# A 31-tap convolution on three engines: ScalarE's tap products against GpSimd and VectorE doing all taps

## The reference, cut to what matters

```python
def hybrid_mix(h, ...):
    p = h @ w_in                               # 21 tiles of 128 channels
    ...
    y_a = gate_b * causal_depthwise_conv(gate_c * xa, sc_conv_w)      # 3 taps
    y_b = spatial_gating(u, v, sg_w, sg_b, sg_ln_w, sg_ln_b)
    y_c = rwkv7_time_mix(pc, ...)
    z1, z2 = jnp.split(pd, 2, axis=-1)
    zd = causal_depthwise_conv(z1 * jax.nn.sigmoid(z2), cm_conv_w) + cm_conv_b   # 31 taps
    y_d = jax.nn.silu(layer_norm(zd, cm_ln_w, cm_ln_b))
    return jnp.concatenate([y_a, y_b, y_c, y_d], axis=-1) @ w_out
```

## Time and profile before

| What | Value |
|---|---|
| median of three executions | 2330.22 us |
| the profiled execution's own time | 2334.19 us |
| its span, first to last instruction | 2332.3 us |
| TensorE busy | 2225.5 us, 95% |
| VectorE busy | 492.4 us, 21% |
| ScalarE busy | 342.0 us, 15% |
| GpSimd busy | 101.4 us, 4% |
| mean granted clock of TensorE | 0.956 of full |
| chain that ended last | PE 92%, DVE 5%, ACT 1% |

### The profile page before, as it was taken

The page is one execution under the profiler, slowest core; times in us unless marked ns, Lnnn a source line. Parts: engine busy times, 40 slices in busy tenths (PEclk is TensorE's granted clock), DMA queues, the critical chain, the costliest instruction groups (busy, mean ns, idle before and its releaser), DMA issues.

```text
span 2332.3 us, 26353 instructions
## 1 busy us (share of the span) xinstructions
PE 2225.5 (95%) x10308; PEld 1757.5 (75%) x10308; DVE 492.4 (21%) x1056; ACT 342.0 (15%) x773; POOL 101.4 (4%) x132
## 2 busy tenths in 40 slices
PE   8978899999878999999999999999999999999998
PEld 6755788888756788877777886877687778867776
DVE  0336310012452200021000463100110015530001
ACT  1113210001111100020000351100110013511001
POOL 0000000000000000000000070000000001600000
PEclk9965999999879999999999999999999999989999
DMA  6410244444202344434444421544464444124443
GB/s 256 149 37 0 73 145 153 153 135 134 93 35 67 114 153 153 150 130 129 151 153 143 148 71 57 178 153 153 145 218 153 153 149 140 63 68 158 153 153 117
DMA packets 81584, 299.47 MB, mean 128 GB/s; under 512 B 9120, under 2 KB 9248, under 8 KB 81248
## 3 DMA queue, kind: packets, MB, share of 16 engines
q1 hardware_dynamic: 80352, 293.87, 38.1%
q0 software_dynamic: 1152, 4.45, 0.5%
HBM read 296.98 MB, written 1.05 MB: 128 GB/s over the span
## 4 chain that ended last, share of the span: by engine, by line
PE 92%; DVE 5%; ACT 1%; issue 1%; DVEq 1%; DMA 0%; ACTq 0%; SPq 0%
PE psum L284 46%; PE psum L469 12%; PE psum L266 10%; PE psum L724 7%; PE psum L1674 5%; PE psum L2161 3%; PE psum L441 2%; PE psum L425 2%; PE psum L1558 1%; PE psum L2479 1%; PE psum L350 1%; PE psum L1622 1%; PE psum L404 0%; DVE sq L578 0%; DVE x L582 0%
## 5 line engine op out<-in xcount | busy, mean ns | idle before, releaser
L284 PE MATMUL psum<-h,ring 128*128 128x256 f32 x2976 | 654.7, 379 | 0.0
L284 PEld LDWEIGHTS psum<-h,ring 128*128 128x128 f32 x2976 | 565.1, 190 | 105.7 <-issue 32.5
L284 PE MATMUL psum<-x,ring 128*128 128x256 f32 x1728 | 391.4, 384 | 17.9 <-ACT x L2510 7.1
L284 PEld LDWEIGHTS psum<-x,ring 128*128 128x128 f32 x1728 | 332.8, 193 | 66.5 <-issue 16.3
L266 PE MATMUL psum<-hid,ring 128*128 128x256 f32 x1024 | 231.1, 379 | 0.0
L266 PEld LDWEIGHTS psum<-hid,ring 128*128 128x128 f32 x1024 | 194.6, 190 | 26.5
L469 PE MATMUL psum<-ring,hid 128*128 128x512 f32 x448 | 201.4, 592 | 0.0
L523 ACT ACTIVATE hid_act<-psum 128x256 f32<-128x256 f32 x88 | 33.8, 384 | 783.1 <-PE psum L284 729.0
L469 PEld LDWEIGHTS psum<-ring,hid 128*128 128x128 f32 x448 | 85.1, 190 | 83.2 <-issue 80.4
L538 DVE TENSOR_TENSOR hid<-psum,hid_act 128x256 f32<-128x256 f32 x56 | 23.8, 425 | 568.8 <-ACT hid_act L523 568.8
L469 PE MATMUL psum<-ring,space 128*128 128x512 f32 x256 | 112.3, 592 | 0.0
(11 more groups left out here) (328 smaller groups left out, 1620.7 us busy)
## 6 DMA issues: line engine op xcount, KB each, us to landing
ring<-in_weights SPq DMA_DIRECT2D x552, 512.0 KB, 3.3
space<-in_gains POOLq DMA_DIRECT2D x6, 512.0 KB, 4.5
const<-in_consts SPq DMA_DIRECT2D x1, 1493.0 KB, 11.0
x<-in_x SPq DMA_DIRECT2D x1, 1024.0 KB, 4.9
out<-x SPq DMA_DIRECT2D x2, 512.0 KB, 2.6
space<-in_params POOLq DMA_DIRECT2D x2, 509.5 KB, 4.5
space<-in_params SPq DMA_DIRECT2D x1, 659.0 KB, 12.0
space<-in_positions SPq DMA_DIRECT2D x1, 128.0 KB, 13.7
```

The lines of the kernel that those rows point to most:

```text
L284: last = pe.matmul(out, unit[:, i, :], rhs[:, i, :], start=(i == 0), stop=(i == KD - 1), skip_group_check=True)
```

## The change

ScalarE's `products` and GpSimd's `add_products` go, with the two semaphores and the product buffers. GpSimd convolves tile 0 alone with the existing helper `conv(s.zs, "cm_conv_w", CMW, s.zd, 1)`: a tensor_scalar (multiply) for the first tap, then for each of 30 taps a tensor_scalar into one of two `pool_t` tiles, a drain and a tensor_tensor add into `zd`; last a drain and a tensor_scalar that adds the bias, which marks the new step `zd`. VectorE does all 31 taps of tile 1. The fifteen new ones stand in the product series: four ahead of the add `n1`, four between `n1` and `n2`, seven between `n2` and `n3`, so the mark `taps` moves there. TensorE waits for `zd` and `taps` where it waited for the adds; VectorE waits for `zd` ahead of `centre("zn", ...)` and no longer waits ahead of `n1`.

```diff
-OWN_TAPS, PRODUCTS = 16, 4
-ADDED = 2 * CMW - OWN_TAPS
+OWN_TAPS = 16
...
-        self.pool = Steps(sem("mixer_convolutions"), "zs0 ya")
-        self.product_ready, self.product_added = sem("tap_products_ready"), sem("tap_products_added")
+        self.pool = Steps(sem("mixer_convolutions"), "zd ya")
...
-        pe.wait_ge(s.product_added, (l + 1) * (ADDED - 1))
+        pe.wait_ge(*at(s.pool, "zd"))
+        pe.wait_ge(*at(s.dve, "taps"))
         channel_sums("zn", "sum", s.zd, 2)
         out_part(2, 0, 0)
...
-    def products(first, last):
...
-        products(0, 5)
         tiles_out(12, 14)
...
-        products(5, 11)
         tiles_out(14, 16)
         square("vn")
-        products(11, 18)
         tiles_out(16, 18)
-        products(18, 22)
         deviation("vn", 1)
-        products(22, 28)
         tiles_out(18, 20)
-        products(28, 33)
         act.wait_ge(*at(s.dve, "decayed"))
         copy_bank(2, flat(s.vn_tok), "v_norm_tok")
-        products(33, 37)
         tiles_out(20, PROJ2)
...
-        products(37, ADDED)
...
-        taps(12, OWN_TAPS).then_inc(*s.dve.mark("taps"))
+        taps(12, OWN_TAPS)
         tiles_out(15, 17)
...
-        dve.wait_ge(s.product_added, (l + 1) * (ADDED - 1))
+        taps(OWN_TAPS, 20)
         add("n1", 6, s.n[0], s.n[1])
+        taps(20, 24)
         add("n2", 6, s.n[1], s.n[0])
+        taps(24, CMW).then_inc(*s.dve.mark("taps"))
         add("n3", 6, s.n[0], s.n[1])
+        dve.wait_ge(*at(s.pool, "zd"))
         centre("zn", s.zd, 2)
...
-        pool.tensor_tensor(s.zs[:, 0, CMW - 1:], s.z[:, 0, :], s.sz[:, 0, :], ALU.mult).then_inc(*s.pool.mark("zs0"))
+        pool.tensor_tensor(s.zs[:, 0, CMW - 1:], s.z[:, 0, :], s.sz[:, 0, :], ALU.mult)
         pool.drain()
         pool.wait_ge(*at(s.dve, "zs1"))
         load_gain(3 * l + 1)
-
-        def add_products(first, last):
...
-        add_products(1, CMW)
-        pool.wait_ge(*at(s.dve, "taps"))
-        add_products(CMW, ADDED)
+        conv(s.zs, "cm_conv_w", CMW, s.zd, 1)
+        pool.drain()
+        pool.tensor_scalar(s.zd[:, 0, :], s.zd[:, 0, :], s.p("cm_conv_b", 0), None, ALU.add).then_inc(
+            *s.pool.mark("zd"))
```

More of the change, by code:

```diff
@@ L630, in __init__ @@
         self.kk_sq = self.m[8][:, 4:8, :].rearrange("p q t -> p (q t)")
-        self.product = self.m[9].rearrange("p q t -> p (q t)").rearrange("p (n t) -> p n t", t=T)
         self.on_tok = self.m[8][:, 0:4, :].rearrange("p q t -> p (q t)").rearrange("p (n c) -> p n c", n=2)
@@ L670, in __init__ @@
         self.dve = Steps(sem("mixer_elementwise"), [
-            "lora_in", "kk_sq", "zs1", "run", "vn.xc", "decayed", "rkr", "taps", "vn", "bonus", "yb",
+            "lora_in", "kk_sq", "zs1", "run", "vn.xc", "decayed", "rkr", "vn", "bonus", "yb",
             *tt("before", "far_st"), *tt("before_ts", "ak", "rb"), *tt("rk"), *tt("n0"), *tt("p2t"), *tt("n1"),
-            *tt("n2"), *tt("n3"), "zn.xc", *tt("x1"), "zn", *tt("x2"), *tt("x3"), "w1", "nw",
+            *tt("n2"), "taps", *tt("n3"), "zn.xc", *tt("x1"), "zn", *tt("x2"), *tt("x3"), "w1", "nw",
             "s0", "u1", "s1", "u2", "on_stats.0", "s2", "on.0", "u3", "yc.0", "on_stats.1", "on.1", "yc.1"])
-        self.pool = Steps(sem("mixer_convolutions"), "zs0 ya")
-        self.product_ready, self.product_added = sem("tap_products_ready"), sem("tap_products_added")
+        self.pool = Steps(sem("mixer_convolutions"), "zd ya")
     def p(self, name, i=None, n=1):
@@ L1408, in second_pool @@
         load_gain(3 * l + 1)
-        def add_products(first, last):
-            for t in range(first, last):
-                tile = int(t >= CMW)
-                pool.wait_ge(s.product_ready, l * ADDED + t + 1)
-                pool.drain()
-                pool.tensor_tensor(s.zd[:, tile, :], s.zd[:, tile, :], s.product[:, t % PRODUCTS, :], ALU.add).then_inc(
-                    s.product_added, 1)
-        add_products(1, CMW)
-        pool.wait_ge(*at(s.dve, "taps"))
-        add_products(CMW, ADDED)
+        conv(s.zs, "cm_conv_w", CMW, s.zd, 1)
+        pool.drain()
+        pool.tensor_scalar(s.zd[:, 0, :], s.zd[:, 0, :], s.p("cm_conv_b", 0), None, ALU.add).then_inc(
+            *s.pool.mark("zd"))
         w.n["even"] += (PROJ2 + 1) // 2
```

## The result

The changed kernel takes 2342.86 us (median; 2335.32 to 2349.07), the kernel before on the same chip 2330.18 us. The ratio is 1.0055 with a 95% interval of 1.0034 to 1.0075, so it is slower by 12.7 us, and by 7.9 to 17.5 us with the interval. The forecast was 2347.0 us, within 2335.5 to 2358. The sign and the mechanism came out; two terms of the sum were mis-sized, and one margin that I had called safe is not there.

The account below looks back on a forecast made before the run. TensorE, busy 95% of the span, was taken as the bound. Per layer 6.7 us of tap lateness and 1.7 us of slower clock, 2 x (6.7 + 1.7) = 16.8 us on 2330.2, gave 2347.0 us, range 2335.5 to 2358.

Parts of the forecast that it names:

- The hand-over hides; removing it is worth nothing: ScalarE's products and GpSimd's adds end 12.3 us before TensorE needs `zd`, so removing them gains nothing.
- faster: Outcome given 2%: only less disturbance of VectorE's `n0` to be gained, half a microsecond a layer.
- Four taps ahead of `n1` are free, four make `n2` late, seven make the sums late: VectorE's product series: no cost ahead of `n1`, `n2` 1.6 us late, TensorE's channel sums 6.7 us late per layer.
- nothing goes round the wait: At TensorE's wait for `taps`: queued work stands behind it and `n3` is equally late, so all 6.7 us count.
- nothing is paid back: Against the rival that TensorE's 1.37 us wait ahead of `x3` absorbs lateness (2333.6 us, 8%): that wait moves along.
- I take 0.88: VectorE's fifteen taps in the product series start 0.88 us apart, the pitch measured beside GpSimd's adds.
- The bare price: Rival, 13%: VectorE's taps meet nothing, pitch 0.56 us, `taps` 3.1 us late; 2336.4 us, or 2340 with the clock.
- 0.50 behind the wait, worth 1.7 us a layer: Behind TensorE's wait for `taps` some 3.4 us of matmuls run at 1.2 instead of 2.4 GHz, costing 1.7 us.
- I take 4.5 us: VectorE slows GpSimd's own convolution by 4.5 us, between bounds of 2.6 and 16.7, giving `zd` at 1394.5 us.
- this still hides: GpSimd's `zd` at 1394.5 us comes before TensorE's need at 1396.53, so it costs nothing.
- `ya` hides: GpSimd's branch a gives `ya` at about 1407 us; TensorE asked at 1407.93 and will ask later, so no cost.
- VectorE while the projections run: zero: GpSimd's earlier start delays VectorE about 1 us during the projections, within slack of 2.9 us or more; no cost.

Follow-up runs that it names:

- GpSimd's part alone: The changed kernel without VectorE's taps 16 to 30 of tile 1, against the kernel before; ratio 1.0005 (0.9990 to 1.0019).
- VectorE's part alone: The kernel before with VectorE doing all taps of tile 1, ScalarE and GpSimd still sharing tile 0; ratio 1.0053 (1.0033 to 1.0074).
- the changed kernel's second profile: The changed kernel run once more without any edit, against the kernel before; ratio 1.0061 (1.0039 to 1.0083).
- The second placement of the taps: The changed kernel with nine taps ahead of VectorE's wait for ScalarE's copy of tile 20, three behind `yb`, three ahead of `n1`; ratio 1.0023.
- taps in idle time, first place: The changed kernel with nine taps between VectorE's waits for ScalarE's tile 20 copy and `spatial`, three behind `yb`, three ahead of `n1`; ratio 1.0037.

## Why the prediction was right, and where its sizes were off

**"The hand-over hides; removing it is worth nothing": right.** 41 us less on ScalarE, and the projections still take 66.00 of 66.00 us; with GpSimd's part alone the time is 1.0005 (0.9990 to 1.0019). The small gain that the forecast named under "faster", half a microsecond a layer at VectorE's `n0`, is there too: S is 0.46 and 0.29 us shorter in that kernel.

**"Four taps ahead of `n1` are free, four make `n2` late, seven make the sums late": right,** step by step: 1.58 us of VectorE's wait left ahead of `n1`, 0.58 us of TensorE's wait for `n2`, 3.74 and 3.96 us for the taps. The second four make the product `n3` at most 0.4 us late, where 1.6 us were forecast; nearly all of the lateness is the seven's. That nothing goes round the wait and nothing is paid back holds too: four taps more cost 2.3 and 2.6 us for 2.6 us.

**"I take 0.88", the tap pitch: the term that was mis-sized.** It measured 0.64 us in the fours (2.55/4) and 0.72 in the seven (5.02/7). The second four took 2.5 instead of 3.5 us, the seven 5.0 instead of 6.1, and `n2` 1.3 instead of 1.5: 2.3 us less, and the 6.7 us of lateness became 4.3 and 4.2. What was off was the choice of the row. The 0.88 stood for taps beside adds that follow each other with a gap of 0.16 us; in the new convolution every second instruction is a multiply, and a multiply hardly slows a tap. That is not all of it: beside adds alone the product series still has 0.73 to 0.75 us a tap, not 0.88. The bare price was at the other end of the range, and the truth near the middle (VectorE's part alone gives 2.5 us of lateness, so GpSimd adds 1.8).

**"0.50 behind the wait, worth 1.7 us a layer": right in kind, and a little small where it comes.** It measured 1.75 (VectorE's part alone) to 2.8 us a layer and is spared by work in the wait. But it comes in some layers and executions and not in others, which the forecast did not say: one layer of two in the first profile, both in the second.

**"I take 4.5 us" for what VectorE costs GpSimd, and "this still hides": half right.** GpSimd's convolution took 62.2 us; with 55.1 undisturbed that is 7.1 us of slowing, inside the bounds of 2.6 and 16.7. TensorE did not wait for it, but only since the taps were later: that part of the forecast came true by luck. It was complete 1392.49 - 1360.78 = 31.71 us behind the `vn` transposes, where the old need is 31.15: 0.56 us late. In the second layer it was 33.41 us, 2.3 us late, with an idle of 3.72 us near its start, which the forecast had not; in the changed kernel's second profile it was 31.5 and 31.6 us. The second placement of the taps shows what such lateness costs. Here the low row, of adds beside VectorE, was too mild a guide: in the first layer's convolution 30 multiplies average 1104 ns where 922 is undisturbed, 5.5 us in all, and 30 adds 758 ns for 727. About 1.2 us of the slowing is by the new taps themselves (30.5 us behind the transposes without them).

**`ya` hides: right.** The gating ended at 1404.78, and TensorE asked for it at 1407.71. "VectorE while the projections run: zero" is right, with 66.00 of 66.00.

**The sum.** With the measured sizes, 4.3 + 4.2 of lateness and 2 to 5 of clock, 10.7 to 13.1 us, beside a measured 12.7. The forecast's 16.8 less the 4.9 us by which its lateness was too long is 11.9; what is left to 12.7 lies within the clock's 2 to 5 us, for which it had 3.4.

Open: what decides whether the clock falls behind the wait of the same length; why taps beside adds lose 0.19 to 0.21 us each in the product series and 0.26 to 0.33 during the projections; why one tap beside the 128x512 add loses 0.84 us; and what GpSimd's idle near the start of its convolution is. No run here tells these.

## What to carry to other kernels

Work is moved to an idle engine for nothing only if each instruction lands ahead of a wait of that engine that is longer than it: VectorE was 78% idle, and fifteen taps of half a microsecond made TensorE 4.3 us late in each layer in one place, while in another it waited for none of them and only for GpSimd, which they had slowed. Before a change takes load off an engine, look whether TensorE waits for it at all; and when the bound is removed, read which wait is next, since here GpSimd, hidden behind the taps till then, was 0.6 and 1.9 us too late. The price of two engines meeting in SBUF depends on which instructions meet, so take it from a row with the same pair.

## What the runs showed of the hardware

- GpSimd's one-input multiply by a per-partition scalar (128x256, 0.92 us undisturbed) is slower than its two-input add (0.73 us), yet it disturbs VectorE less (0.02 to 0.07 us a tap instead of 0.19 to 0.33) and is itself stretched, up to 1.99 us.
- The granted clock fell behind a wait of 2.63 us in both layers of one kernel and behind one of 2.23 us in another (taps in idle time, first place), and stayed at 1.00 behind one of 3.74 us; it stayed up in all four layers where TensorE had constant matmuls to do. A fall cost 1.6 to 2.8 us.
- A float32 matmul of 128x512 shows as two records of about 0.44 us each, 0.88 us together.
